# Odd layer's output product: first half of its columns spread over attention's last steps, with its weight splits inside attention

## The chip, the cores and the metric

The kernel runs on one core of one Trainium2 chip. The metric is the device time of one execution in microseconds (us). TensorE (PE), VectorE (DVE), ScalarE (ACT), GpSimd (POOL) and SyncE (SP, which here only issues DMAs) run side by side, each in the order of its own program, and meet through semaphores.

## What is computed

Two blocks of a model over 512 tokens of width 1024, in fp32. The change concerns the odd layer of the first block: differential attention with 8 heads, a normalization of each head's output, and the output product, after which comes the MLP.

```python
def diff_mixer(h, w_in, lam, subln_g, w_out, cos, sin, lambda_init):
    q, k, v = jnp.split(proj, 3, axis=-1)          # 8 heads x 2 x 64, rope on q and k
    ...
    def block(i):
        s = jnp.einsum('bqhcd,bshcd->bhcqs', qb, k) * scale
        p = masked_softmax(s, key_pos[None, :] <= tq[:, None])
        a = p[:, :, 0] - lam_val * p[:, :, 1]
        return jnp.einsum('bhqs,bshe->bqhe', a.astype(v.dtype), v)
    o = sweep_query_blocks(block, T)
    o = rms_norm(o, subln_g) * (1.0 - lambda_init)
    return jnp.einsum('bte,ed->btd', o.reshape(bsz, T, ODD_MIX), w_out)

# in first_block, layer 1
h = h + diff_mixer(...)
h = h + sq_relu_mlp(rms_norm(h, mlp_norm_g[layer]), mlp_w_up[layer], mlp_w_down[layer])
```

## The kernel before

Every fp32 product is made of three matmuls of a shorter type: each operand is split into a high part and a rest, and `products` (its matmul is line 367) adds high x high, high x low and low x high in a PSUM bank. A weight piece of 512 rows by 512 columns is loaded by SP into one of two staging buffers (`stg0`, `stg1`), ACT copies it to `wh` (L341), and DVE subtracts to get `wl` (L345). There are two `wh`/`wl` pairs too. So the split of a piece waits until TensorE has signalled "free" for the piece two before it. `split(e, key, ahead=1)` issues the split of the named piece and of the next one on engine `e`, if they haven't been issued yet. All of this stands in program order on ACT and DVE: what is behind a split waits for it.

**Attention.** 32 units n = 0 to 31: head `n // 4`, and block of 128 query rows `n % 4`, whose scores are 128, 256, 384 or 512 wide. It runs in 40 steps. In step n TensorE does, in this order: a filler, if there is one; `pe_diff_out` of unit n-3 (L1778), `pe_rows_turn` of a head, if it is due (L1828), `pe_diff_flip` of unit n-2 (L1758, transposes), `pe_diff_scores` of unit n (L1716 and the causal mask L1718). DVE takes the maximum of unit n (L1725) at the end of its step n, ACT the exponential (L1738) in step n+1, DVE the probabilities (L1746, L1748, L1750) in step n+1, ACT copies the transposed ones (L1766) in step n+2. Scores use PSUM banks 0 to 2 in turn, so those of unit n wait for exponentials of units n-2 and n-1.

**The rows of a head.** When the last unit of head hh is out, ACT squares the head (L1802, step 4hh+7), DVE sums (L1807, L1809, step 4hh+8), POOL raises to -1/2 (L1814), DVE scales (L1821, 4hh+9), TensorE transposes (L1828, 4hh+10), ACT copies the high part (L1834, 4hh+10), DVE the rest (L1838, 4hh+11). Its signal is `("rows", hh)`. The output product of head hh can start then. Head hh+2 uses the same PSUM bank, so its first `pe_diff_out` also waits for `("rows", hh)`. Below, turn(hh), copy(hh) and rest(hh) are the last three of these operations.

**Fillers.** Up to step 25 the filler is a piece of the projection of later heads (`pe_dr`), 12 matmuls in most steps. The last of it ends in step 25. After that the filler is the output product `pe_out1`: its first half of columns, c = 0, is 4 row tiles (i) by 8 heads by 3 matmuls. The heads 0 to 3 are weight piece (0,0), the heads 4 to 7 piece (0,1); the second half of columns has pieces (1,0) and (1,1). Before the change `next(out1)` gives one tile of the heads 0 to 3, 12 matmuls, in each of the steps 28, 30, 33 and 34. The heads 4 to 7 of all tiles, 48 matmuls, come after step 39: they wait for `("rows", 7)` and for the split of piece (0,1), which ACT and DVE reach only behind the rows of head 7, at the start of `act_add_norm` and `dve_add_norm`.

**Behind it.** `pe_add_norm` then runs the second half of columns in the order (heads 0 to 3: tiles 0, 1), (heads 4 to 7: tiles 0, 1), (heads 0 to 3: tiles 2, 3), (heads 4 to 7: tiles 2, 3), and the transposes of the norm. DVE adds each finished bank to `h` (L579), ACT squares it (L547). Piece (1,1) is split behind the squares of tiles 0 to 2 on ACT, when piece (0,1) is free.

Of the kernel before, what the change touches and what calls it, by code (L numbers as in the profile page):

```python
# [18 lines left out]
NT = 4  # L19
# [96 lines left out]
def build(nc, ins, out):  # L116
    ctx = ExitStack()
    with ctx:
# [10 lines left out]
        banks = ctx.enter_context(nc.psum_tensor("banks", [128, 8, 512], F32))[:, :, :]  # L129
        bank = [banks[:, i, :] for i in range(8)]  # L130
# [3 lines left out]
        rows = sb("rows", [NROWS, 128])  # L134
# [41 lines left out]

        BANKS = {"out0": (7, 0, 1, 2, 3, 4, 5, 6), "out1": (6, 7, 0, 1, 2, 3, 4, 5), "out2": (0, 1, 2, 3, 4, 5, 6, 7)}
        for tag, source in (("mlp0", "out0"), ("mlp1", "out1"), ("mlp2", "out2")):  # L180
            BANKS[tag] = BANKS[source][4:] + BANKS[source][:4]
        NORMS = {"n1": ("out0", "mlp_norm_g", 0), "n2": ("mlp0", "mix_norm_g", 8), "n3": ("out1", "mlp_norm_g", 8),
# [143 lines left out]
        def split(e, key, ahead=1):  # L326

            last = ORDER.index(key) + ahead
            while at_split[e] <= min(last, len(ORDER) - 1):
                k = ORDER[at_split[e]]  # L330
                at_split[e] += 1
                if SPEC[k][3]:
                    continue
                n = SPLITS.index(k)
                hi, lo = halves_of(k)
                if e == "act":
                    act = engine[e]
                    act.wait_ge(*piece_in[ORDER.index(k) % 2].at(k))
                    if n >= 2:
                        act.wait_ge(*p_mm.at(("free", SPLITS[n - 2])))  # L340
                    act.activation(hi, stage_of(k), ACT.Copy).then_inc(*a_hi.next(k))  # L341
                else:
                    dve = engine[e]
                    dve.wait_ge(*a_hi.at(k))
                    dve.tensor_tensor(lo, stage_of(k), hi.bitcast(F32), ALU.subtract).then_inc(*v_lo.next(k))  # L345
# [106 lines left out]
        def pe_add(pe, tag, lhs, nk, ready, free, banks=range(8), cs=range(2)):  # L452
            for c in cs:
                for g in range(nk // 4):
                    key = tag + (c, g)
                    wh, wl = take(pe, key)
                    ready(pe, g)
                    for i in range(NT):
                        if g == 0:
                            free(pe, c, i)  # L460
                        t = products(pe, bank[banks[c * 4 + i]], [(*lhs(g * 4 + k, i), wh[:, k, :], wl[:, k, :]) for k in range(4)],
                                     g == 0, g == nk // 4 - 1)
                        names = [(tag, c, i)] if g == nk // 4 - 1 else []
                        if i == NT - 1:
                            names.append(("free", key))
                        if names:
                            t.then_inc(*p_mm.next(*names))
                        yield
# [17 lines left out]

        def pe_add_norm(pe, tag, lhs, ready, free, norm, banks):
            yield from pe_add(pe, tag, lhs, 8, ready, free, banks, (0,))  # L490
            w = {}
            for x, (g, i) in enumerate(((0, 0), (0, 1), (1, 0), (1, 1), (0, 2), (0, 3), (1, 2), (1, 3))):
                if i == 0:
                    w[g] = take(pe, tag + (1, g))
                if g == 0:
                    free(pe, 1, i)
                wh, wl = w[g]
                t = products(pe, bank[banks[4 + i]], [(*lhs(g * 4 + k, i), wh[:, k, :], wl[:, k, :]) for k in range(4)],
                             g == 0, g == 1)
                names = ([(tag, 1, i)] if g else []) + ([("free", tag + (1, g))] if i == 3 else [])  # L500
                if names:
                    t.then_inc(*p_mm.next(*names))
                if norm in NORMS and x in (4, 5):
                    pe_turned(pe, norm, x - 4)
                yield
# [1215 lines left out]
        def dve_diff_max(dve, n):  # L1721
            hh, i = DIFF[n]
            for c in range(2):
                dve.wait_ge(*p_score.at(("diff", n, c)))
                dve.tensor_reduce(small[n % 16][:, c:c + 1], diff_bank(n, c)[:, 0:(i + 1) * 128], AX.X, ALU.max,  # L1725
                                  negate=True).then_inc(*v_max.next(("diff", n, c)))
# [34 lines left out]
        def act_diff_flip(act, n):  # L1761
            hh, i = DIFF[n]
            act.wait_ge(*p_flip.at(("diff", n)))
            if n >= 2:
                act.wait_ge(*p_out.at(("diff", n - 2)))
            act.activation(TDD[n % 2][:, 0:(i + 1) * 128], bank[3][:, 0:(i + 1) * 128], ACT.Copy).then_inc(  # L1766
                *a_flip.next(("diff", n)))
# [17 lines left out]
        def rows_at(n, step):  # L1785
            hh, off = divmod(n - step, 4)
            return hh if off == 0 and 0 <= hh < 8 else None
# [36 lines left out]
        def pe_rows_turn(pe, hh):  # L1824
            pe.wait_ge(*v_norm.at(("rows", hh)))
            for i in range(NT):
                s = slice(i * 128, (i + 1) * 128)
                t = pe.transpose(head_bank(hh)[:, s], OQ[:, hh % 2, s], ident)  # L1828
            t.then_inc(*p_flip.next(("rows", hh)))
# [14 lines left out]
        def first(steps, n):  # L1844
            for _ in range(n):
                next(steps, None)

        def pe_diff(pe):

            N = len(DIFF)  # L1850
            dr, out1 = pe_dr(pe), pe_out1(pe)
            first(dr, AHEAD)
            for n in STEPS:
                next(dr, None)
                if n in (N - 4, N - 2, N + 1, N + 2):
                    next(out1)
                if 0 <= n - 3 < N:
                    pe_diff_out(pe, n - 3)
                if rows_at(n, TURN) is not None:
                    pe_rows_turn(pe, rows_at(n, TURN))  # L1860
                if 0 <= n - 2 < N:
                    pe_diff_flip(pe, n - 2)
                if n < N:
                    pe_diff_scores(pe, n)
                yield
            yield from out1

        def act_diff(act):
            N = len(DIFF)
            dr, pieces = act_dr(act), act_dr_pieces(act)  # L1870
            for _ in range(AHEAD):
                first(dr, 1)
                first(pieces, 1)
            for n in STEPS:
                next(dr, None)
                if 0 <= n - 1 < N:
                    act_diff_exp(act, n - 1)
                next(pieces, None)
                if rows_at(n, SQUARE) is not None:
                    act_rows_square(act, rows_at(n, SQUARE))  # L1880
                if rows_at(n, TURN) is not None:
                    act_rows_turn(act, rows_at(n, TURN))
                if 0 <= n - 2 < N:
                    act_diff_flip(act, n - 2)
                yield

        def dve_diff(dve):
            N = len(DIFF)
            dr = dve_dr(dve)
            first(dr, AHEAD)  # L1890
            for n in STEPS:
                if rows_at(n, REST_OF) is not None:
                    dve_rows_rest(dve, rows_at(n, REST_OF))
                if 0 <= n - 1 < N:
                    if n == 1:
                        dve.wait_ge(*v_misc.at("lambda"))
                    dve_diff_prob(dve, n - 1)
                next(dr, None)
                if rows_at(n, TOTAL) is not None:
                    dve_rows_total(dve, rows_at(n, TOTAL))  # L1900
                if rows_at(n, SCALE) is not None:
                    dve_rows_scale(dve, rows_at(n, SCALE))
                if n < N:
                    dve_diff_max(dve, n)
                yield

        def pool_diff(pool):
            dr = pool_dr(pool)
            first(dr, AHEAD)
            for n in STEPS:  # L1910
# [2 lines left out]
                    pool_rows_total(pool, rows_at(n, TOTAL))  # L1913
                yield

        def pe_out1(pe):
            def lhs(k, i):
                return oTh[:, k, i * 128:(i + 1) * 128], oTl[:, k, i * 128:(i + 1) * 128]

            def ready(pe, g):  # L1920
                pe.wait_ge(*v_part.at(("rows", g * 4 + 3)))

            def free(pe, c, i):
                if c:
                    pe.wait_ge(*v_part.at(("rows", 7)))
                elif i < 2:
                    pe.wait_ge(*v_rope.at("dq7"))
                else:
                    pe.wait_ge(*a_exp.at(("diff", 31, 1)))
            return pe_add_norm(pe, ("out1",), lhs, ready, free, "n3", BANKS["out1"])  # L1930


        (nq, nk, nv, nbr), at = regions(0, [128, 4, T], [128, 4, T + 2 * META], [128, 4, T], [128, 2, 896])
# [1170 lines left out]
```

## Time and profile before

| | us |
|---|---|
| median of 3 runs | 2292.42 (2287.23 to 2292.9) |
| profiled execution | 2297.29 |
| its span on the core | 2295.5 |
| TensorE busy in the span | 2186.1 (95%) |
| DVE busy | 1058.2 (46%) |
| ACT busy | 766.3 (33%) |
| from the end of step 26 to the end of the first half of columns (964.96 to 1024.60) | 59.64, TensorE busy 44.62 |

Times within the span are counted from its start. A matmul of 512 columns shows about 0.39 us, but its successor starts 0.23 us after it, since they are pipelined; a row of the chain of waits ("x12") gives the time that the group really took. The profile's TensorE clock is 1.00 at 2.4 GHz and 0.50 at 1.2 GHz.

### The profile page before, as it was taken

The page shows a single profiled execution, that of the slowest core. Times are in us where ns is not written, and L with a number is a line of the kernel's source. Part 1 is how long each engine was busy: PE and PEld are TensorE (multiplying, and loading weights), DVE is VectorE, ACT ScalarE, POOL GpSimd, SP SyncE. Part 2 cuts the span into 40 slices and gives each one's busy share as a digit, 9 for nine tenths or more (in the row PEclk, how much of TensorE's full clock was granted, in tenths as well). Part 3 has the DMA queues.
Part 4 walks back from the last instruction along what each step waited for, and adds up shares of the span by engine and source line. Part 5 has one row for each costly group of instructions (what it writes and reads, how often), then busy time and mean ns, then how long its engine had stood idle before and what let it go on. Part 6 is the DMA issues. An engine that isn't in the chain of part 4 may idle for free.

```text
span 2295.5 us, 26641 instructions
## 1 busy us (share of the span) xinstructions
PE 2186.1 (95%) x10987; PEld 1729.6 (75%) x10987; DVE 1058.2 (46%) x1590; ACT 766.3 (33%) x1254; POOL 332.4 (14%) x308
## 2 busy tenths in 40 slices
PE   6978888999999999989999999999999999999998
PEld 5765557888888776668888888866778768888887
DVE  3568853433333456744333335355656434333333
ACT  3215453432232334434322324133423224423221
POOL 2210000111010011101200102111155320201000
PEclk9989989999999999989999999999999999999999
DMA  5430001332322321112232233221112214222321
GB/s 139 113 92 19 20 1 55 101 101 92 102 100 92 93 76 38 38 51 87 97 105 92 92 110 92 90 72 53 56 45 67 74 40 135 92 94 95 106 92 73
DMA packets 163506, 182.60 MB, mean 80 GB/s; under 512 B 19701, under 2 KB 123562, under 8 KB 163386
## 3 DMA queue, kind: packets, MB, share of 16 engines
q1 hardware_dynamic: 161066, 174.11, 24.2%
q0 software_dynamic: 2320, 6.80, 1.2%
q8 instruction: 87, 1.43, 0.3%
q14 instruction: 33, 0.27, 0.0%
HBM read 177.75 MB, written 2.17 MB: 78 GB/s over the span
## 4 chain that ended last, share of the span: by engine, by line
PE 86%; DVE 7%; ACT 3%; issue 2%; DMA 1%; SPq 1%; POOL 0%; POOLq 0%; ACTq 0%; DVEq 0%
PE banks L367 70%; PE banks L2482 2%; DVE wl L345 2%; ACT wh L341 2%; PE banks L1272 1%; PE banks L1192 1%; PE banks L1308 1%; PE banks L2601 1%; DVE uTl L537 1%; PE banks L1716 1%; PE banks L1778 1%; PE banks L2222 1%; PE banks L2172 1%; PE banks L2251 1%; PE banks L1640 1%
## 5 line engine op out<-in xcount | busy, mean ns | idle before, releaser
L367 PE MATMUL banks<-uTh,wh 128*128 128x512 f32 (+1 forms) x1408 | 555.0, 394 | 13.9 <-DVE wl L345 4.2
L367 PE MATMUL banks<-uTl,wh 128*128 128x512 f32 (+1 forms) x1408 | 539.7, 383 | 0.0
L367 PE MATMUL banks<-uTh,wl 128*128 128x512 f32 (+1 forms) x1408 | 539.6, 383 | 0.0
L367 PE MATMUL banks<-wh,hTr 128*128 128x512 f32 x1696 | 532.1, 392 | 5.5 <-DVE wl L345 4.9
L345 DVE TENSOR_TENSOR wl<-stg,wh 128x2048 fp32r<-128x2048 f32 (+1 forms) x154 | 357.2, 2320 | 385.1 <-ACT wh L341 384.6
L341 ACT ACTIVATE wh<-stg 128x2048 fp32r<-128x2048 f32 (+1 forms) x154 | 292.7, 1902 | 432.0 <-PE banks L367 399.6
L367 PEld LDWEIGHTS banks<-wh,hTr 128*128 128x128 f32 x1696 | 321.0, 189 | 73.2 <-DVE wl L345 5.3
L367 PE MATMUL banks<-wl,hTr 128*128 128x512 f32 x848 | 331.9, 391 | 0.0
L367 PEld LDWEIGHTS banks<-uTh,wh 128*128 128x128 f32 x1408 | 269.0, 191 | 70.3 <-issue 10.1
L367 PEld LDWEIGHTS banks<-uTh,wl 128*128 128x128 f32 x1408 | 268.3, 191 | 52.6
L367 PEld LDWEIGHTS banks<-uTl,wh 128*128 128x128 f32 x1408 | 269.2, 191 | 50.2 <-issue 2.4
L709 POOL TENSOR_TENSOR p<-p 128x512 f32<-128x512 f32 x96 | 109.9, 1144 | 667.5 <-ACT p L697 667.5
L720 DVE TENSOR_TENSOR hTr<-p,hTr 128x512 fp32r<-128x512 f32 x96 | 66.4, 692 | 303.2 <-ACT hTr L701 303.2
L367 PEld LDWEIGHTS banks<-wl,hTr 128*128 128x128 f32 x848 | 160.7, 190 | 33.2
L697 ACT ACTIVATE p<-banks 128x512 f32<-128x512 f32 x96 | 57.6, 600 | 202.9 <-PE banks L367 202.9
L367 PE MATMUL banks<-wh,uTh 128*128 128x512 f32 (+1 forms) x256 | 100.7, 393 | 9.9 <-DVE wl L345 6.3
L701 ACT ACTIVATE hTr<-p 128x512 fp32r<-128x512 f32 x96 | 60.7, 632 | 120.5 <-POOL p L709 120.5
L367 PE MATMUL banks<-wh,uTl 128*128 128x512 f32 (+1 forms) x256 | 98.6, 385 | 0.0
L367 PE MATMUL banks<-wl,uTh 128*128 128x512 f32 (+1 forms) x256 | 98.5, 385 | 0.0
L483 DVE TENSOR_TENSOR h<-h,banks 128x512 f32<-128x512 f32 x72 | 49.4, 686 | 82.9 <-PE banks L367 82.9
L444 POOL TENSOR_TENSOR nrm<-nrm,half 128x1 f32<-128x1 f32 x28 | 15.5, 554 | 490.8 <-DVE nrm L591 468.3
L367 PEld LDWEIGHTS banks<-wh,uTh 128*128 128x128 f32 x256 | 48.8, 190 | 20.8 <-DVE wl L345 7.0
(362 smaller groups left out, 2282.8 us busy)
## 6 DMA issues: line engine op xcount, KB each, us to landing
stg<-mlp_w_up SPq DMA_DIRECT2D x32, 1024.0 KB, 5.4
stg<-mlp_w_down SPq DMA_DIRECT2D x32, 1024.0 KB, 5.0
stg<-w_in SPq DMA_DIRECT2D x20, 1024.0 KB, 5.2
stg<-w_up SPq DMA_DIRECT2D x16, 1024.0 KB, 5.3
stg<-w_down SPq DMA_DIRECT2D x16, 1024.0 KB, 5.0
stg<-odd_w_in SPq DMA_DIRECT2D x16, 512.0 KB, 4.7
stg<-even_cmp_w SPq DMA_DIRECT2D x4, 1024.0 KB, 5.5
stg<-odd_w_in SPq DMA_DIRECT2D x4, 1024.0 KB, 5.1
```

Source lines behind the costliest of these rows:

```text
L341: act.activation(hi, stage_of(k), ACT.Copy).then_inc(*a_hi.next(k))
L345: dve.tensor_tensor(lo, stage_of(k), hi.bitcast(F32), ALU.subtract).then_inc(*v_lo.next(k))
L367: t = pe.matmul(outp, x, y, start=(start and k == 0 and m == 0), stop=(stop and k == n - 1 and m == 2))
L483: dve.tensor_tensor(hc, hc, bank[banks[c * 4 + i]], ALU.add).then_inc(*v_add.next((tag, c, i)))
L537: dve.scalar_tensor_tensor(out=uTl[:, k, s], in0=norm_rows(norm, ph, k), scalar=col(gname, g0 + k), in1=uTh[:, k, s].bitcast(F32), op0=ALU ...
L697: act.activation(P[n % 5][:, 0:T], bank[BANKS[tag][j]], ACT.Relu).then_inc(*a_up.next((tag, "relu", q, j)))
L701: act.activation(HT[q % 2][0][:, j, :], P[n % 5][:, 0:T], ACT.Copy).then_inc(*a_up.next((tag, "hi", n)))
L709: pool.tensor_tensor(r, r, r, ALU.mult).then_inc(*g_up.next((tag, n)))
L720: dve.tensor_tensor(HT[q % 2][1][:, j, :], P[n % 5][:, 0:T], HT[q % 2][0][:, j, :].bitcast(F32), ALU.subtract).then_inc(*v_up.next((tag, n)))
L1192: pe.matmul(b[:, g, :], qv[p, j, i * 128:(i + 1) * 128], kv[p, 0:w], start=True, stop=False)
L1272: t = pe.transpose(b[:, g, s], p[:, g, s], ident)
L2482: t = pe.matmul(b, fill_w["y"][:, k, f * 128:(f + 1) * 128], (onT, ohT)[br][:, k, :], start=(k == 0), stop=(k == 3))
```

## The change

- `pe_out1_half` replaces the first half of columns. The heads 0 to 3 now go in portions of 6 matmuls (two heads of a tile) or 3 (one head): tile 0 in steps 27 and 28, tile 1 in steps 29 (head 0), 30 (head 1) and 31 (heads 2, 3), tile 2 in steps 32 and 33, tile 3 in steps 34 and 35.
- The heads 4 to 6 go in 4 portions of 9 matmuls, tile 0 to 3, in steps 35 to 38. They wait for `("rows", 6)`. In step 38 the portion stands behind the transposes of head 7.
- Head 7 comes last: 4 portions of 3 matmuls, which wait for `("rows", 7)`.
- Piece (0,1) is split at the end of step 29 on ACT and DVE, piece (1,0) at the end of step 36.
- Tiles 2 and 3 change banks (1 and 0 instead of 0 and 1), and each tile waits only for what used its own bank: tile 2 for the exponential of unit 30, tile 3 for that of unit 31.

The number of matmuls stays the same.

```diff
@@ pe_diff
-                if n in (N - 4, N - 2, N + 1, N + 2):
+                if N - 5 <= n < N + 3:
                     next(out1)
                 if 0 <= n - 3 < N:
                     pe_diff_out(pe, n - 3)
                 if rows_at(n, TURN) is not None:
                     pe_rows_turn(pe, rows_at(n, TURN))
+                if N + 3 <= n < N + 7:
+                    first(out1, 2 if n == N + 3 else 1)
@@ act_diff, and the same in dve_diff, as the last thing of a step
+                if n in OUT1_SPLITS:
+                    split("act", OUT1_SPLITS[n])
@@
+        OUT1_SPLITS = {len(DIFF) - 3: ("out1", 0, 0), len(DIFF) + 4: ("out1", 0, 1)}
+        def pe_out1_half(pe):
+            w = take(pe, ("out1", 0, 0))
+            pe.wait_ge(*v_part.at(("rows", 3)))
+            for i in range(NT):
+                if i == 0:
+                    pe.wait_ge(*a_rope.at("dq7"))
+                elif i == 1:
+                    pe.wait_ge(*v_rope.at(("dq7", "sin")))
+                else:
+                    pe.wait_ge(*a_exp.at(("diff", 30 if i == 2 else 31, 1)))
+                for heads in ((0,), (1,), (2, 3)) if i == 1 else ((0, 1), (2, 3)):
+                    t = part(w, i, heads)
+                    if i == NT - 1 and heads[-1] == 3:
+                        t.then_inc(*p_mm.next(("free", ("out1", 0, 0))))
+                    yield
+            w = take(pe, ("out1", 0, 1))
+            pe.wait_ge(*v_part.at(("rows", 6)))
+            for i in range(NT):
+                part(w, i, (4, 5, 6))
+                yield
+            pe.wait_ge(*v_part.at(("rows", 7)))
+            for i in range(NT):
+                t = part(w, i, (7,))
+                t.then_inc(*p_mm.next((("out1",), 0, i), *([("free", ("out1", 0, 1))] if i == NT - 1 else [])))
+            yield
```

TensorE, between the scores of step 26 and those of step 27 (`wh0`, `wl0` are piece (0,0); `hTr_49` holds the normalized heads; `+` is the change):

```order
 L1716 MATMUL banks<-big 128x384 x2
 L1718 MATMUL banks<-causal,identb 128x128 x2
+L367 MATMUL banks<-wh0,hTr_49 128x512
+L367 MATMUL banks<-wl0,hTr_49 128x512
+L367 MATMUL banks<-wh0,hTr_49 128x512 x2
+L367 MATMUL banks<-wl0,hTr_49 128x512
+L367 MATMUL banks<-wh0,hTr_49 128x512
 L1778 MATMUL banks<-big 128x128
 L1758 MATMUL banks<-k_c_ident,p 128x128 x2
```

The first six matmuls of the output product moved to here, ahead of the `pe_diff_out` of unit 24, where nothing stood before.

TensorE, at the end of attention, steps 34 and 35 (`wh1` is piece (0,1)):

```order
 L1778 MATMUL banks<-big 128x128 x4
-L1828 MATMUL banks<-k_c_ident,big 128x128 x8
+L1828 MATMUL banks<-k_c_ident,big 128x128 x4
+L367 MATMUL banks<-wh0,hTr_49 128x512
+L367 MATMUL banks<-wl0,hTr_49 128x512
+L367 MATMUL banks<-wh0,hTr_49 128x512 x2
+L367 MATMUL banks<-wl0,hTr_49 128x512
+L367 MATMUL banks<-wh0,hTr_49 128x512
 L367 MATMUL banks<-wh1,hTr_49 128x512
 L367 MATMUL banks<-wl1,hTr_49 128x512
```

Before, the transposes of the heads 6 and 7 stand next to each other (x8); now product work stands between them, and those of head 7 come in step 38, ahead of the last portion of heads 4 to 6.

DVE, the ends of steps 29 and 36 (`sm13` belongs to unit 29; L345 is a split, `wl1` that of piece (0,1), `wl0` that of piece (1,0)):

```order
 L1821 TENSOR_TENSOR big<-banks,nrm 128x512
 L1725 TENSOR_REDUCE sm13<-banks 128x1 x2
+L345 TENSOR_TENSOR wl1<-stg1,wh1 128x2048
 L1746 RECIPROCAL sm13<-sm13 128x2
 L1748 TENSOR_SCALAR big<-big,sm13 128x256
@@ -679,8 +680,7 @@
 L1807 TENSOR_REDUCE nrm<-q1 128x4
 L1809 TENSOR_SCALAR nrm<-nrm 128x4
+L345 TENSOR_TENSOR wl0<-stg0,wh0 128x2048
 L1821 TENSOR_TENSOR big<-banks,nrm 128x512
 L1838 SCALAR_TENSOR_TENSOR hTr_49<-banks,big,hTr_49 128x512
-L345 TENSOR_TENSOR wl1<-stg1,wh1 128x2048
-L345 TENSOR_TENSOR wl0<-stg0,wh0 128x2048
```

Both splits moved from behind the last rest (L1838) to two places inside attention: one ahead of the probabilities of unit 29, one ahead of the scaling of head 7. On ACT they moved likewise, ahead of the exponentials of unit 29 and ahead of the copy of head 7.

## Rows read from the trace of the kernel before

**Rows 1.** The page, its first line: span and instructions.

```profile
span 2295.5 us, 26641 instructions
```

**Rows 2.** Stretches: length, then busy us of each engine, PEclk, DMA share, GB/s.

```profile
964.96:1024.60 59.64, 44.62 (x199) 33.71 (x199) 28.47 (x51) 19.53 (x46) 3.02 (x3) 0.80 0.11 36
...
988.00:990.00 2.00, 2.00 (x11) 1.34 (x8) 1.35 (x3) 0.36 (x2) 0.00 (x0) 0.64 0.00 0
...
994.00:996.00 2.00, 2.00 (x8) 1.59 (x7) 0.69 (x1) 0.00 (x0) 0.62 (x1) 0.65 0.00 0
...
1006.00:1008.00 2.00, 0.56 (x3) 0.16 (x1) 0.68 (x1) 1.40 (x2) 0.00 (x0) 0.50 0.00 0
```

**Rows 3.** Chain of waits, end of attention: start, us, engine, tile, line, count.

```profile
1001.38 0.70 ACT hTr L1834
...
1003.72 1.02 POOL nrm L1814
...
1005.51 1.06 PE banks L1828 x4
...
1007.18 1.91 ACT wh L341
...
1009.12 2.30 DVE wl L345
...
1011.46 26.83 PE banks L367 x108
```

**Rows 4.** TensorE in order of time: start, us, line, operation, [idle before, releaser].

```profile
962.91 0.65 PE L1828 MATMUL banks<-k_c_ident,big 128*128 128x128 f32 x4 [0.65 <-DVE big L1821]
...
968.54 0.76 PE L1778 MATMUL banks<-big 128*128 128x128 f32 x2 [3.58 <-DVE hTr L1838]
...
986.98 0.46 PE L1778 MATMUL banks<-big 128*128 128x128 f32 x2 [1.81 <-DVE hTr L1838]
...
1015.89 0.40 PE L367 MATMUL banks<-wl,hTr 128*128 128x512 f32 x1
```

**Rows 5.** Chain of waits, steps 30 to 33, where the product is a filler.

```profile
979.84 2.83 PE banks L367 x12
982.67 0.89 PE banks L1778 x8
983.56 0.44 PE banks L1828 x4
...
991.22 4.93 PE banks L367 x12
```

**Rows 6.** DVE in order of time, around the ends of steps 29 to 31.

```profile
979.67 0.68 DVE L1821 TENSOR_TENSOR big<-banks,nrm 128x512 f32<-128x512 f32 x1
980.28 0.74 DVE L1725 TENSOR_REDUCE sm<-banks 128x1 f32<-128x256 f32 x2
981.78 0.17 DVE L1746 RECIPROCAL sm<-sm 128x2 f32<-128x2 f32 x1 [0.76 <-ACT big L1738]
...
982.43 0.49 DVE L1750 SCALAR_TENSOR_TENSOR big<-big,sm 128x256 f32<-128x256 f32 x1
985.15 1.02 DVE L1725 TENSOR_REDUCE sm<-banks 128x1 f32<-128x384 f32 x2 [2.23 <-PE banks L1718]
986.09 0.74 DVE L1838 SCALAR_TENSOR_TENSOR hTr<-banks,big,hTr 128x512 fp32r<-128x512 f32 x1
```

**Rows 7.** ACT in order of time: a square, its accumulator, split of (1,1).

```profile
1022.73 0.63 ACT L547 ACTIVATE q<-h 128x512 f32<-128x512 f32 x1 [2.00 <-DVE h L579]
1023.27 0.19 ACT L547 ACTIVATION_READ_ACCUMULATOR q<-h 128x1 f32 x1
1024.79 1.92 ACT L341 ACTIVATE wh<-stg 128x2048 fp32r<-128x2048 f32 x1 [1.33 <-PE banks L367]
```

**Rows 8.** DVE in order of time: last add of the first half, split of (1,1).

```profile
1024.73 0.69 DVE L579 TENSOR_TENSOR h<-h,banks 128x512 f32<-128x512 f32 x1 [2.03 <-PE banks L367]
1026.74 2.29 DVE L345 TENSOR_TENSOR wl<-stg,wh 128x2048 fp32r<-128x2048 f32 x1 [1.32 <-ACT wh L341]
```

More of the change, by code:

```diff
@@ L175, in build @@
         xn = [PF[:, 0:D], PF[:, D:2 * D], TF[:, 0:D], TF[:, D:2 * D]]
-        BANKS = {"out0": (7, 0, 1, 2, 3, 4, 5, 6), "out1": (6, 7, 0, 1, 2, 3, 4, 5), "out2": (0, 1, 2, 3, 4, 5, 6, 7)}
+        BANKS = {"out0": (7, 0, 1, 2, 3, 4, 5, 6), "out1": (6, 7, 1, 0, 2, 3, 4, 5), "out2": (0, 1, 2, 3, 4, 5, 6, 7)}
         for tag, source in (("mlp0", "out0"), ("mlp1", "out1"), ("mlp2", "out2")):
@@ L484, in dve_add, with pe_add_norm @@
                     yield
-        def pe_add_norm(pe, tag, lhs, ready, free, norm, banks):
-            yield from pe_add(pe, tag, lhs, 8, ready, free, banks, (0,))
+        def pe_add_norm(pe, tag, lhs, ready, free, norm, banks, half=None):
+            yield from half or pe_add(pe, tag, lhs, 8, ready, free, banks, (0,))
             w = {}
@@ L1904, in dve_diff @@
                     dve_diff_max(dve, n)
+                if n in OUT1_SPLITS:
+                    split("dve", OUT1_SPLITS[n])
                 yield
@@ L1914, in pool_diff, with part @@
                 yield
+        OUT1_SPLITS = {len(DIFF) - 3: ("out1", 0, 0), len(DIFF) + 4: ("out1", 0, 1)}
+        def pe_out1_half(pe):
+            banks = BANKS["out1"]
+            def part(w, i, heads):
+                wh, wl = w
+                return products(pe, bank[banks[i]], [(*out1_rows(k, i), wh[:, k % 4, :], wl[:, k % 4, :]) for k in heads],
+                                heads[0] == 0, heads[-1] == 7)
+            w = take(pe, ("out1", 0, 0))
[22 more added lines that the diff above has]
+            yield
@@ L1916, in pe_out1, with out1_rows @@
+        def out1_rows(k, i):
+            return oTh[:, k, i * 128:(i + 1) * 128], oTl[:, k, i * 128:(i + 1) * 128]
         def pe_out1(pe):
-            def lhs(k, i):
-                return oTh[:, k, i * 128:(i + 1) * 128], oTl[:, k, i * 128:(i + 1) * 128]
             def ready(pe, g):
-                pe.wait_ge(*v_part.at(("rows", g * 4 + 3)))
+                pe.wait_ge(*v_part.at(("rows", 7)))
             def free(pe, c, i):
[L1924 to L1929, printed above, removed]
@@ L1930, in pe_out1 @@
-            return pe_add_norm(pe, ("out1",), lhs, ready, free, "n3", BANKS["out1"])
+                pe.wait_ge(*v_part.at(("rows", 7)))
+            return pe_add_norm(pe, ("out1",), out1_rows, ready, free, "n3", BANKS["out1"], pe_out1_half(pe))
         (nq, nk, nv, nbr), at = regions(0, [128, 4, T], [128, 4, T + 2 * META], [128, 4, T], [128, 2, 896])
```

## The prediction

> **What bounds the kernel now.** The page first: one execution spans 2295.5 us [rows 1], and TensorE is busy for 95% of it, so what can be won lies where TensorE waits or runs at its low clock. The view by stretches finds such a place: from the end of step 26 (964.96) to the end of the output product's first half (1024.60) pass 59.64 us, of which TensorE works 44.62 at a mean clock of 0.80 [rows 2]. It idles for 15.0 us, and the clock takes a share as well.
>
> The timeline of TensorE shows where it idles. In step 27 it waits 3.58 us and in step 31 1.81 us, both times ahead of the first `pe_diff_out` of a head, for rest(4) and rest(5) on DVE [rows 4]. The largest part comes at the end. The chain of waits reads: copy(6), rest(6) and the sums of head 7, POOL's power, the scaling, turn(7) at 1005.51, then ACT's split of piece (0,1) for 1.91 us and DVE's for 2.30 us, and only then 108 matmuls in a row from 1011.46 [rows 3]. That last link is the one to see: rest(7) isn't in the chain; the split is. From 1001.34 (end of turn(6)) to 1011.46 TensorE works 1.06 us.
>
> The clock: it is at 0.50 (1.2 GHz) in three spells, each behind idle time. The first runs from the work resumed at 968.54 to about 975, the second from about 988.7 (0.64 in the stretch 988 to 990) to about 995.4 (0.65 in 994 to 996), the third from about 1005.8 to 1015.89 (0.50 in 1006 to 1008) [rows 2, 4]. Twelve matmuls take 2.83 us at the full clock (0.23 each, taken for all portions below) and 4.93 mostly at the low one (0.43 each) [rows 5]. The excess of work done low is 3.1 us in the first spell (6.5 us of work), 3.1 in the second (6.8 less 0.56 of waiting, halved), and 2.6 in the third: 1.06 us of transposes, and ten matmuls until 1015.89 for which 4.43 us pass instead of 2.3. Together 8.8 us.
>
> The Trainium skill, "TensorE: Matmul & The Clock Gate", section Terms, gives the penalty of the low clock as the throttled time times (1 - K/N), here a half. By the stretches the clock was low for 0.20 x 59.64 / 0.50 = 23.9 us, so that rule would book 11.9 us where the rows give 8.8; the difference is idle time at the low clock, mostly in the third spell. Since the third spell goes entirely, the gain would be 2.5 us larger by the rule.
>
> **The change, step by step.** The matmuls are the same in number, and I assume that a portion of 6 costs 1.4 us. Starting a portion might cost up to 0.09 us (2.83 for x12 against 12 x 0.23) [rows 5]; four more portions stand in the steps, so between 0 and 0.4 us; I take 0 since most start behind other matmuls, and keep 0.4 for the range. I take the change through the steps against the ends of the steps before.
>
> Step 27: the first 6 matmuls run from 964.96 to 966.4, in the wait. Rest(4) on DVE is bound by DVE's own queue and doesn't move, so `pe_diff_out` still starts at 968.54 and the step ends at 971.8 as before. The idle time is 2.1 us, more than the 1.81 behind which the clock fell before [rows 4], so I let the first spell stand.
> Step 28 has 6 matmuls instead of 12, at the low clock: it ends at 976.2 instead of 977.6. Step 29 has 3 new ones and ends at 978.9 (before 979.7). Step 30 has 3 instead of 12: 0.7 + 0.89 + 0.44 [rows 5] + 1.1 for transpose and scores, to 982.1 (before 985.1). The lead is 3 us.
>
> Step 31 takes part of it back, because of the split of piece (0,1). ACT starts it behind the copy of unit 27 (978.65, as TensorE's transposes of it end at 978.0) and ends at 980.6; DVE is done with the maximum of unit 29 at 980.15 (0.74 from 979.4 [rows 6]), waits, and splits from 980.6 to 982.9. Before, DVE waited 0.76 and 2.23 us between that maximum and the next one [rows 6], so most of the 2.30 us would be covered at the old pace; at the new one it isn't. Behind the split come the probabilities of unit 29 (1.15 from 981.78 to the end of 982.43's row), the maximum of unit 30 (0.92) and rest(5) (0.74) [rows 6]: 985.7. TensorE has finished its 6 matmuls at 983.5 and waits 2.2 us for it. The step ends at 987.5 instead of 988.9. Without the split rest(5) would be ready at 983.8.
> An idle time of 2.2 us is again above 1.81, so I let a second spell of 6.6 us stand too, 1.7 us after the work resumes as before. Steps 32 and 33 (6 matmuls each, two outs, two flips) then end at 991.6 and 995.2. The exponential of unit 31 isn't waited for: its portion comes only in step 34. Before, step 33 ended at 997.2 and step 34 at 1001.34; now step 34 (6 matmuls, 8 for out, turn(6)) ends at 998.0. Lead 3.3 us.
>
> Steps 35 to 38: 6 matmuls to 999.4; rest(6) is there 1.5 us after turn(6) (0.70 [rows 3] + 0.74 [rows 6]), at 999.5. Then 9 matmuls each, to 1001.6, 1003.7 and 1005.7. Beside it runs the chain of head 7: squares to 999.3, sums to 1000.4, power 1.02 to 1001.5 [rows 3]. The split of piece (1,0) can start on ACT when (0,0) is free, at 999.4, and ends at 1001.35; DVE's ends at 1003.7, and the scaling of head 7 queued behind it ends at 1004.4 instead of 1002.2. This costs nothing, since TensorE comes to turn(7) at 1005.7. Cover: 1.3 us. Turn(7) to 1006.2, 9 matmuls to 1008.2, in which copy(7) and rest(7) (1.5 us) fit. Head 7's 12 matmuls end at 1011.0.
> Before, the 48 matmuls from 1011.46 ended at 1024.6. **Sum: 1024.6 - 1011.0 = 13.6 us.** By kinds: 15.0 us idle becomes 4.5 (2.1, 2.2, 0.15), and 8.8 us of low clock become 6.2: 13.1, with 0.5 left to rounding.
>
> What comes behind: the second half of columns starts at once with piece (1,0), split long ago. Piece (1,1) is needed after 24 matmuls, 5.5 us behind. Before, its split began with the free signal and DVE ended it 4.4 us behind 1024.6 (1026.74 + 2.29) [rows 8]. Now all four adds come in a burst of 2.1 us of matmuls, and ACT makes three squares of 0.8 us (0.63 and 0.19, overlapping a little [rows 7]) first, each behind an add (0.69 [rows 8]): the split starts 1.05 us behind, is done on ACT at 2.95 and on DVE at 5.25. The margin is 0.2 us; I take 0, at most 1. The rest of the program keeps its order.
>
> **Rivals.** *The clock holds better*: with 1.4 us of work in either wait, one of the two spells stays out, 3.1 us each: gain 16.7, or 19.8 for both. For it: step 26's wait of 0.65 us brought no spell. Against it: 1.81 us did [rows 4]. Times 2275.7 and 2272.6.
> *A split comes into the path after all*: ACT and DVE's 1.91 + 2.30 = 4.2 us [rows 3] show in full, either before turn(7), where 1.3 us cover them, or at (1,1), or in steps 30 and 31, where ACT's split also stands ahead of the exponential of unit 29 that the scores of unit 30 need. Once: gain 9.4, 2283.0; twice: 5.2, 2287.2.
> *Nothing*: the splits or products don't get their data in time and TensorE waits as before, since its chain to rest(7) rules: 2292.
> *Slower, by the clock*: the portions are short and lie between transposes and narrow products; if TensorE stays at 1.2 GHz from 968.54 on, the 33.6 us of full-clock work up to the end of the half take 67.2 and end at 1035.7, 11.1 us later than before: 2303.5. It turns the sign only if the low clock lasts 27 us longer than the 13 that I have reckoned. Before, spells in the same mix of instructions ended after 6.5 us [rows 2], so this is unlikely.
>
> **How the numbers follow.** The sum is made against the profiled execution (span 2295.5, 2297.29 in all, 1.79 outside the span). Its time is 4.87 above the median of the runs shown; the gain is in one stage and is carried over whole: 2292.42 - 13.6 = 2278.8. Chances: forecast 0.50, clock holds better 0.20, split in the path 0.20 (a quarter of it at the second price), nothing 0.05, slower 0.05. About 0.3%, 6.9 us, is what a measurement of this kernel can tell from no change. So faster 0.85, same 0.10, slower 0.05. The range leaves out "nothing" and "slower" and takes in the others: 2271 (both spells gone, 1.6 for the spread of the runs) to 2287.
>
> **What would show it.** In the profile of the changed kernel: L367 directly behind the scores of step 26; a wait of about 2 us ahead of L1778 in step 27 and of about 2 in step 31, with an L345 shortly before on DVE; no idle above 0.5 us between turn(6) and the end of the second half of columns; no split in the chain of waits between L1828 and the long row of L367; two low spells, none behind 1000. From 964.96 to the end of the first half it should be 46.0 us instead of 59.6. The prediction is wrong if TensorE waits for L345 at head 4 or at piece (1,1), if turn(7) waits for the scaling, or if a third spell shows.

## The result, and the profile after

| | before | after |
|---|---|---|
| median of 4 runs | 2291.86 us (2287.23 to 2292.90) | 2275.20 us (2268.36 to 2277.46) |
| span of the profiled execution | 2295.5 | 2274.4 |
| stage: end of step 26 to the end of the first half of columns | 59.64 | 42.75 |
| TensorE busy in the stage | 44.62 | 38.33 |

The changed kernel takes 0.9926 of the time before (95% interval 0.9901 to 0.9952): 16.7 us less by the medians, where 13.6 were forecast. A later comparison of the same kernel on another occasion gave 0.9935 (0.9918 to 0.9952).

The two profiled executions lie 21.1 us apart. The view by stretches (length, busy us of each engine, PEclk, DMA share, GB/s) of the changed kernel, cut in three, shows which part is the change:

```profile
0.00:961.05 961.05, 889.84 (x4703) 690.29 (x4708) 487.43 (x859) 345.01 (x660) 106.66 (x108) 0.97 0.26 76
961.05:1003.80 42.75, 38.33 (x198) 28.87 (x198) 28.12 (x51) 18.55 (x44) 3.02 (x3) 0.96 0.16 50
1003.80:2274.40 1270.60, 1246.61 (x6084) 1002.19 (x6083) 540.85 (x682) 403.27 (x553) 223.79 (x197) 0.99 0.26 85
```

The middle line answers to the first of [rows 2] and holds 16.9 of the 21.1 us. What follows takes 1270.6 us, and took 1270.9 (2295.5 - 1024.6) before. The first stretch is 3.9 us shorter (961.05 against 964.96), in code that the change doesn't touch: it is scatter of single executions (the same stretch takes 959.21 us in the run below whose code up to there is that of before, and between 956.6 and 963.7 in the others), and the medians don't carry it.

In the stage, TensorE's timeline (start, us, line, operation, idle before and its releaser) shows every gap that is left:

```profile
964.62 0.46 PE L1778 MATMUL banks<-big 128*128 128x128 f32 x2 [2.13 <-DVE hTr L1838]
...
979.53 0.46 PE L1778 MATMUL banks<-big 128*128 128x128 f32 x2 [2.02 <-DVE hTr L1838]
...
992.14 0.47 PE L367 MATMUL banks<-wh,hTr 128*128 128x512 f32 x1 [0.26 <-DVE hTr L1838]
...
998.38 0.60 PE L1828 MATMUL banks<-k_c_ident,big 128*128 128x128 f32 x4
```

The first two answer to [rows 4] with its 3.58 and 1.81 us; the 0.26 is the wait for rest(6); turn(7) has no wait at all. The chain of waits (start, us, what) at the same place, against [rows 3]:

```profile
990.52 0.70 ACT hTr L1834
...
991.24 0.76 DVE hTr L1838
...
992.14 6.40 PE banks L367 x27
998.54 0.44 PE banks L1828 x4
998.98 18.42 PE banks L367 x81
```

At the end of attention POOL, the scaling and both splits have left it: behind rest(6) there is only TensorE, up to the norm. One split is still in the chain, further ahead. From step 27 to the wait in step 31 the chain runs mostly through DVE and ACT and holds no filler (no L367), and both halves of the split of piece (0,1) are links of it:

```profile
972.63 1.81 ACT wh L341
...
974.46 2.29 DVE wl L345
```

TensorE also waits once where its timeline shows no gap, since short waits inside a group count as busy. The scores of unit 29 took 0.70 us before (first line) and take 1.32 in the change (second line), at the same clock:

```profile
978.92 0.70 PE L1716 MATMUL banks<-big 64*128 64x256 f32 x4
...
971.21 1.32 PE L1716 MATMUL banks<-big 64*128 64x256 f32 x4
```

The second pair of them needs a bank that unit 28 used, and the profile names the exponential (L1738) as what TensorE waits for there. TensorE comes earlier to it than before, as the low spell of step 27 is gone.

### The profile page after: what moved, and what is told of

Same layout as the page of the kernel before. It is cut to its first block, busy times and chain, and to the rows that moved or that the text cites. A ratio compares the mean times of both kernels' runs of the same rounds, so it can differ in the third digit from the quotient of the medians.

```text
span 2274.4 us, 26637 instructions
## 1 busy us (share of the span) xinstructions
PE 2174.8 (96%) x10983; PEld 1721.4 (76%) x10987; DVE 1056.4 (46%) x1590; ACT 766.8 (34%) x1254; POOL 333.5 (15%) x308
## 4 chain that ended last, share of the span: by engine, by line
PE 86%; DVE 8%; ACT 3%; issue 2%; DMA 1%; SPq 1%; POOL 0%; POOLq 0%; ACTq 0%; DVEq 0%
PE banks L367 70%; PE banks L2519 2%; DVE wl L345 2%; ACT wh L341 2%; PE banks L1272 1%; PE banks L1192 1%; PE banks L1308 1%; PE banks L2638 1%; DVE uTl L537 1%; PE banks L1716 1%; PE banks L1778 1%; PE banks L2209 1%; PE banks L2288 1%; PE banks L1640 1%; PE banks L2259 1%
## 5 line engine op out<-in xcount | busy, mean ns | idle before, releaser
L367 PE MATMUL banks<-uTh,wh 128*128 128x512 f32 (+1 forms) x1408 | 554.2, 394 | 14.1 <-DVE wl L345 4.2
L367 PE MATMUL banks<-uTl,wh 128*128 128x512 f32 (+1 forms) x1408 | 539.0, 383 | 0.0
L367 PE MATMUL banks<-uTh,wl 128*128 128x512 f32 (+1 forms) x1408 | 538.9, 383 | 0.0
L345 DVE TENSOR_TENSOR wl<-stg,wh 128x2048 fp32r<-128x2048 f32 (+1 forms) x154 | 355.4, 2308 | 382.6 <-ACT wh L341 381.9
L367 PE MATMUL banks<-wh,hTr 128*128 128x512 f32 x1696 | 530.5, 391 | 0.3 <-DVE hTr L1838 0.3
L367 PEld LDWEIGHTS banks<-wh,hTr 128*128 128x128 f32 x1696 | 318.9, 188 | 66.7 <-issue 0.7
L367 PE MATMUL banks<-wl,hTr 128*128 128x512 f32 x848 | 330.5, 390 | 0.0
L367 PEld LDWEIGHTS banks<-uTh,wh 128*128 128x128 f32 x1408 | 268.0, 190 | 70.9 <-issue 10.3
L367 PEld LDWEIGHTS banks<-uTh,wl 128*128 128x128 f32 x1408 | 267.2, 190 | 52.5
L367 PEld LDWEIGHTS banks<-uTl,wh 128*128 128x128 f32 x1408 | 268.1, 190 | 50.2 <-issue 2.4
L367 PEld LDWEIGHTS banks<-wl,hTr 128*128 128x128 f32 x848 | 159.5, 188 | 32.6
L367 PE MATMUL banks<-wh,uTh 128*128 128x512 f32 (+1 forms) x256 | 100.4, 392 | 10.9 <-DVE wl L345 6.3
L367 PE MATMUL banks<-wh,uTl 128*128 128x512 f32 (+1 forms) x256 | 98.3, 384 | 0.0
L367 PE MATMUL banks<-wl,uTh 128*128 128x512 f32 (+1 forms) x256 | 98.2, 384 | 0.0
L367 PEld LDWEIGHTS banks<-wh,uTh 128*128 128x128 f32 x256 | 48.6, 190 | 21.8 <-DVE wl L345 7.0
```

The lines of the kernel that those rows point to most:

```text
L367: t = pe.matmul(outp, x, y, start=(start and k == 0 and m == 0), stop=(stop and k == n - 1 and m == 2))
```

## Experiments

All profiles are compared over the same code. "Stage" is as above. "Long stretch" is from the scores of step 26 (L1716, 384 wide) to the first transposes of the norm (L517): 963.60 to 1038.13, so 74.53 us, before; 959.68 to 1017.24, so 57.56, in the change. A few us of one stage are at or below what the device time can tell, so the verdicts rest on profiles, and the device times stand beside them.

**The change once more.**

> The change as it is, beside the others. The stage from the end of step 26's scores to the end of the output product's first half took 59.6 us before and 42.8 after. Theory (waits of TensorE on DVE, and the low clock behind them): the stage stays at 42 to 46 us, with a wait of 2.0 to 2.2 us in step 27 and one in step 31; each may or may not bring a low spell of up to 3 us more. Rival (the 3.1 us by which the change beat the forecast of 46.0 is scatter of this one profile): a second profile shows about 46.

Measured: 2276.5 us, long stretch 57.54. The stage by stretches:

```profile
959.09:1001.80 42.71, 38.28 (x198) 28.82 (x198) 28.11 (x51) 18.51 (x44) 3.02 (x3) 0.96 0.16 50
```

It repeats to 0.04 us, with waits of 2.13 and 2.04. So 42.7 is what the change takes, and the 3 us below the forecast need a cause.

**Only the splits moved.** The kernel before, with this added at the end of the steps of ACT and DVE:

```diff
+                if n in OUT1_SPLITS:
+                    split("act", OUT1_SPLITS[n])
...
+                if n in OUT1_SPLITS:
+                    split("dve", OUT1_SPLITS[n])
...
+        OUT1_SPLITS = {len(DIFF) - 3: ("out1", 0, 0), len(DIFF) + 4: ("out1", 0, 1)}
```

These are the steps 29 and 36, as in the change.

> The kernel before, with only the two splits moved (end of steps 29 and 36); TensorE's order is that of before. Theory: a split isn't worth its own length. Piece (0,1) is ready early, but the split of (1,0) now holds the scaling of head 7 up by about 2 us with nothing on TensorE to cover it, and the 48 matmuls start behind rest(7): 59.6 - 3.4 + 2.0, a stage of 58 to 59 us, a gain of 1 to 2. Rival (the wait for the split was the cost that the change takes away): 4.2 to 4.9 us less, a stage of 55.

Measured: ratio 1.0001 (0.9991 to 1.0012), stage 58.69. TensorE's timeline at the end, against [rows 3]:

```profile
1001.42 1.11 PE L1828 MATMUL banks<-k_c_ident,big 128*128 128x128 f32 x4 [5.99 <-DVE big L1821]
1004.19 0.77 PE L367 MATMUL banks<-wh,hTr 128*128 128x512 f32 x1 [1.66 <-DVE hTr L1838]
```

The split that stood in the chain for 4.2 us is gone, and 1.0 us is all that comes of it. The wait ahead of turn(7) grew from 4.17 to 5.99 us, because the split of (1,0) now stands ahead of the scaling, and the start then waits 1.66 for rest(7). The theory's sum holds; the rival falls.

**Heads 4 to 6 behind head 7's transposes.** In the change:

```diff
-                if N + 3 <= n < N + 7:
-                    first(out1, 2 if n == N + 3 else 1)
+                if n == N + 3:
+                    next(out1)
```

> The change with one part undone: the four portions of heads 4 to 6 are no longer in steps 35 to 38 but behind step 39, ahead of head 7's. Splits and the portions of steps 27 to 35 stay. Theory: TensorE then waits for the chain of head 7 (squares, sums, power, split of (1,0), scaling, transposes, copy, rest), about 5 us ahead of turn(7) and 1.5 behind it, and a low spell follows: stage 50 to 52 us. Rival (the filling of steps 27 to 34 carries the gain, the end would be covered anyway): 43 to 45.

Measured: ratio 0.9963 (0.9948 to 0.9978), stage 49.30:

```profile
998.23 1.12 PE L1828 MATMUL banks<-k_c_ident,big 128*128 128x128 f32 x4 [4.99 <-DVE big L1821]
```

The stage by stretches:

```profile
962.40:1011.70 49.30, 40.15 (x198) 30.22 (x198) 28.14 (x51) 18.55 (x44) 3.02 (x3) 0.90 0.13 43
```

The wait of 5 us is there as forecast. The 1.5 us behind turn(7) are not: the heads 4 to 6 need only rest(6), and run directly after it. So the placement in steps 35 to 38 is worth 6.6 us of the 16.9, not 7.3 to 9.3. The rival falls too.

**Nothing in step 27.** In the change:

```diff
-                if N - 5 <= n < N + 3:
-                    next(out1)
+                if N - 4 <= n < N + 3:
+                    first(out1, 2 if n == N - 4 else 1)
```

> The change with one part undone: nothing in step 27, two portions of six in step 28. Theory: the wait in step 27 is 3.6 us again, a low spell follows it as before, and the 1.4 us of matmuls come on top in step 28: stage 1.4 + about 3 us longer than that of the change, 46.5 to 48. Rival (the low spells come at random and don't depend on the length of the wait): only the 1.4 us, 44.2.

Measured: ratio 0.9955 (0.9940 to 0.9970), stage 46.05. The stage and the 6.5 us behind the wait, by stretches:

```profile
961.70:1007.75 46.05, 40.22 (x198) 30.27 (x199) 28.32 (x51) 18.64 (x44) 3.02 (x3) 0.89 0.14 46
965.28:971.80 6.52, 6.52 (x19) 4.07 (x20) 3.34 (x8) 2.32 (x6) 0.00 (x0) 0.56 0.01 3
```

The wait is 3.58 us again and the low clock (0.56) is back behind it. The stage is 3.3 us longer, 0.5 below the range: 1.4 of it is idle time (the six matmuls don't fill the wait) and 1.9 busy time. The spell itself costs 2.6 us: from 965.28 to 972.53 pass 7.25 us, and the same matmuls take 1.77 + 2.86 = 4.6 at a clock of 1.00. In return the scores of unit 29 take 0.70 us again instead of 1.32, since TensorE comes later. That the spell came back speaks for the theory, and the next run tests it at another length.

In step 31 TensorE waits 1.99 us in this run, and a second spell follows, as in the change:

```profile
983.51 0.46 PE L1778 MATMUL banks<-big 128*128 128x128 f32 x2 [1.99 <-DVE hTr L1838]
```

The stretch from 986 to 988, where the clock (third number from the end) is 0.50:

```profile
986.00:988.00 2.00, 2.00 (x6) 1.61 (x6) 1.26 (x2) 1.30 (x4) 0.00 (x0) 0.50 0.00 0
```

**Three matmuls in step 27.** Tile 0 goes as heads 0, 1, (2, 3), one of them in step 27, two in step 28:

```diff
-                for heads in ((0,), (1,), (2, 3)) if i == 1 else ((0, 1), (2, 3)):
+                for heads in ((0,), (1,), (2, 3)) if i < 2 else ((0, 1), (2, 3)):
...
-                    next(out1)
+                    first(out1, 2 if n == N - 4 else 1)
```

> The change with 3 matmuls in step 27 and 9 in step 28. The wait in step 27 is then about 2.8 us, between the 2.1 of the change (no low spell) and the 3.6 of the kernel before (a low spell of 6.5 us). Theory (a longer wait brings the spell): it comes back, at 2.8 us, and the stage takes 45 to 46 us. Rival (what stands behind the wait decides, not its length up to 3.5): no spell, 43.4.

Measured (one run, 2282.5): stage 44.15. TensorE's timeline of steps 27 and 31:

```profile
967.23 0.77 PE L1778 MATMUL banks<-big 128*128 128x128 f32 x2 [2.82 <-DVE hTr L1838]
...
985.12 0.46 PE L1778 MATMUL banks<-big 128*128 128x128 f32 x2 [1.99 <-DVE hTr L1838]
```

Stretches of 2 us behind either of them:

```profile
969.00:971.00 2.00, 2.00 (x7) 0.63 (x4) 0.31 (x1) 0.00 (x0) 0.00 (x0) 0.50 0.00 0
...
987.00:989.00 2.00, 2.00 (x14) 1.74 (x13) 1.29 (x2) 1.22 (x3) 0.00 (x0) 1.00 0.00 0
```

At 2.82 us the spell is there again, so in this step it comes at 2.82 and 3.58 us and not at 2.13. A shorter wait always has more matmuls ahead of it here (0, 3 or 6), so these runs don't tell the length of the wait from the work before it. The stage is between the two expectations, since the second spell, behind the 1.99 us of step 31, stayed out this time. The run before had the same 1.99 us at the same place, ahead of the same matmuls, and the spell came; so it did behind the 2.02 us of the change. So the length of the wait doesn't decide alone, and what else does is open.

**The split of piece (0,1) in step 31.** In the change:

```diff
-        OUT1_SPLITS = {len(DIFF) - 3: ("out1", 0, 0), len(DIFF) + 4: ("out1", 0, 1)}
+        OUT1_SPLITS = {len(DIFF) - 1: ("out1", 0, 0), len(DIFF) + 4: ("out1", 0, 1)}
```

> The change with the split of piece (0,1) at the end of step 31 instead of 29; all else as in the change (stage 42.7 us in two profiles). Theory: the wait of 2.0 us in step 31 is caused by that split, which stands ahead of the probabilities of unit 29, the maximum of unit 30 and rest(5) on DVE. Behind step 31 the split fits in, since DVE waits there for the exponential of unit 31. Then the wait falls to about 0.3 us and the low spell behind it goes too: stage 39.5 to 40.5. Rival (DVE is full in these steps, so the split costs its 2.3 us wherever it stands): the wait moves to flip(31) or turn(6), stage 42 to 43.

Measured: ratio 0.9932 (0.9914 to 0.9950), 2276.5 us; stage 40.56, 0.06 above the theory's range. TensorE's timeline of steps 31 and 33:

```profile
977.59 0.46 PE L1778 MATMUL banks<-big 128*128 128x128 f32 x2 [0.56 <-DVE hTr L1838]
...
984.52 0.66 PE L1758 MATMUL banks<-k_c_ident,p 128*128 128x128 f32 x4 [0.71 <-DVE p L1750]
```

The stage by stretches:

```profile
960.64:1001.20 40.56, 36.90 (x198) 27.99 (x198) 28.03 (x51) 18.51 (x44) 3.02 (x3) 1.00 0.16 53
```

The wait in step 31 falls from 2.02 to 0.56 us and the clock stays at 1.00. Part of the split shows elsewhere, 0.71 us ahead of flip(31), as the rival said, but a third only. So that wait was for the most part the split's, and the place costs 2.2 us of stage (0.8 of idle time and 1.4 of low clock). The device time doesn't show it (2276.5 us, against 2275.2 and 2276.5 in the two comparisons of the change): 2 us are 0.1%. This profile also gives the stage's busy time at full clock, in the change's order: 36.9 us. It includes the 0.6 us of waiting inside the scores of unit 29.

**And step 27 filled.** Beside that:

```diff
-                for heads in ((0,), (1,), (2, 3)) if i == 1 else ((0, 1), (2, 3)):
+                for heads in ((0, 1, 2, 3),) if i == 0 else ((0,), (1,), (2, 3)) if i == 1 else ((0, 1), (2, 3)):
...
-                if N - 5 <= n < N + 3:
+                if N - 5 <= n < N + 3 and n != N - 2:
```

> As split_31, and tile 0 goes whole (12 matmuls) into step 27, tile 1's portions into steps 28, 29 and 31; step 30 has none. Theory: the matmuls that fill the wait in step 27 (2.1 us with six of them) are taken from steps in which TensorE doesn't wait, so 1.4 us come off: stage 38 to 39.2. Rival (with less filler in steps 28 and 30 TensorE waits there for exponentials): as split_31, 39.5 to 40.5.

Measured: ratio 0.9933 (0.9916 to 0.9949), 2275.5 us; stage 40.55. TensorE's timeline of steps 27, 29 and 31:

```profile
961.33 0.46 PE L1778 MATMUL banks<-big 128*128 128x128 f32 x2 [0.77 <-DVE hTr L1838]
...
968.55 0.70 PE L1716 MATMUL banks<-big 64*128 64x256 f32 x2 [0.20 <-ACT p L1738]
...
974.71 0.46 PE L1778 MATMUL banks<-big 128*128 128x128 f32 x2 [0.74 <-DVE hTr L1838]
```

The wait in step 27 fell by 1.4 us and the stage by nothing. The scores of unit 29 now wait for an exponential, step 31 waits 0.2 us more, and the busy time is 0.8 us longer at the same clock (37.7 against 36.9), in short waits that don't show as gaps: the rival was right. From step 27 to the flip of unit 31 the chain of waits of either profile holds no filler: the loop of scores, maximum, exponential and probabilities is the bound there. That is why this filler could be moved without effect.

**The split of piece (1,0) behind attention again.** In the change, `OUT1_SPLITS = {len(DIFF) - 3: ("out1", 0, 0)}`.

> The change with the second split undone: piece (1,0) is split behind rest(7) again, at the start of add_norm, not in step 36. Measured from the scores of step 26 to the first norm transposes (74.5 us before, 57.6 in two profiles of the change). Theory: on TensorE it is needed at once, so about 0.4 us of waiting there, and DVE's adds and with them the split of (1,1) come 2.3 us later than in the change, where that split had 0.5 us to spare: 1.7 us more. Together 59.5 to 60. Rival (head 7's portions and the second half's first 24 matmuls cover it): 57.6 to 58.

Measured (one run, 2276.1): long stretch 956.33 to 1015.53, so 59.20, 1.6 us more. TensorE's timeline at the first matmul with piece (1,1):

```profile
1007.23 0.50 PE L367 MATMUL banks<-wh,hTr 128*128 128x512 f32 x1 [0.94 <-DVE wl L345]
```

The last matmul of the first half and the first with piece (1,0) make a pair that takes 0.99 us instead of 0.62, because DVE isn't done with that piece:

```profile
1000.03 0.99 PE L367 MATMUL banks<-wh,hTr 128*128 128x512 f32 x2
```

Both waits of the theory are there: 0.4 us at the start of the second half, as expected, and 0.94 at (1,1) instead of 1.7. So the sum is a little below (1.6 instead of 1.9 to 2.4). The early split serves the next split, of (1,1), more than its own piece.

**Tile 2 waits for unit 31 again.** In the change, `pe.wait_ge(*a_exp.at(("diff", 31, 1)))` for tiles 2 and 3.

> The change with one part undone: tile 2, in step 32, waits for the exponential of unit 31, as before the change, though its bank was last used by unit 30. Theory: TensorE stands for about 2.1 us in step 32 (its portion starts there at 981.8, the exponential ends at 983.9), with out(29) and flip(30) queued behind, so the stretch from step 26's scores to the first norm transposes grows by 1.5 to 3 us to 59 to 60.5. Rival (the exponential of unit 31 holds the steps anyway, in flip(31)): 57.6.

Measured (one run, 2278.2): long stretch 955.23 to 1015.65, so 60.42, 2.9 us more:

```profile
979.63 0.79 PE L367 MATMUL banks<-wh,hTr 128*128 128x512 f32 x1 [2.15 <-ACT big L1738]
```

The wait is 2.15 us as computed, and the low spell lasts 6.8 us instead of 3.4, the wait included. So the finer wait is a needed part of the change. It rests on the exchange of banks, which this run leaves as it is in the change: by the code, the bank that tile 2 had before is one of unit 31's.

## Why the prediction was right, and where it was off

**The bound and the sum of idle time.** Right. 15.0 us of idle time became 42.75 - 38.33 = 4.4, forecast 4.5, in the places named: 2.13 in step 27 (2.1), 2.02 in step 31 (2.2), 0.26 for rest(6) (0.15). In step 31 both sides of the wait came earlier than forecast, TensorE by 2.1 us and DVE by 2.4, counted from the end of step 26, because the first low spell was missing; so the wait between them came out nearly as reckoned.

**Step 31 and the split.** Right, and shown by the run with the split in step 31. The chain goes as forecast: ACT's half of the split, DVE's half, the probabilities of unit 29, the maximum of unit 30, rest(5). DVE's timeline in the change, against [rows 6]:

```profile
973.62 0.75 DVE L1725 TENSOR_REDUCE sm<-banks 128x1 f32<-128x256 f32 x2
974.46 2.29 DVE L345 TENSOR_TENSOR wl<-stg,wh 128x2048 fp32r<-128x2048 f32 x1
...
977.71 1.02 DVE L1725 TENSOR_REDUCE sm<-banks 128x1 f32<-128x384 f32 x2
978.64 0.74 DVE L1838 SCALAR_TENSOR_TENSOR hTr<-banks,big,hTr 128x512 fp32r<-128x512 f32 x1
```

From the maximum of unit 29 to rest(5) there is no gap, where DVE waited 0.76 and 2.23 us before.

**Steps 35 to 38.** Right: the scaling, held up by the split of (1,0), ended 1.6 us ahead of turn(7) (at 996.8; forecast 1.3), and head 7's matmuls didn't wait. Undoing this placement costs 6.6 us, undoing the early split of (1,0) alone 1.6, at the start of the second half and at (1,1). The margin there was 0.5 us instead of 0.2. The first half ends at 1003.8, so piece (1,1) is needed at 1009.3, and DVE is done with it at 1008.7:

```profile
1006.44 2.29 DVE L345 TENSOR_TENSOR wl<-stg,wh 128x2048 fp32r<-128x2048 f32 x1 [1.92 <-ACT wh L341]
```

**The clock: the step that was off.** The prediction let both spells stand, "2.1 us, more than the 1.81 behind which the clock fell before". The first spell stayed out in all six profiles with a wait of 2.13 us in step 27, and the second lasted 3.4 us instead of 6.6. Stretches of the change behind step 27's wait and behind step 31's:

```profile
966.00:968.00 2.00, 2.00 (x12) 1.45 (x11) 1.29 (x2) 0.71 (x3) 0.00 (x0) 1.00 0.04 8
...
980.00:982.00 2.00, 2.00 (x9) 0.67 (x8) 0.90 (x3) 0.41 (x2) 0.00 (x0) 0.68 0.62 242
982.00:984.00 2.00, 2.00 (x6) 1.59 (x6) 1.25 (x2) 1.31 (x4) 0.00 (x0) 0.50 0.00 0
984.00:986.00 2.00, 2.00 (x13) 1.74 (x12) 1.76 (x4) 0.63 (x3) 0.00 (x0) 0.97 0.00 0
```

The 36.9 us that the changed order takes at full clock, less the 0.6 us of waiting in the scores of unit 29, are 36.3 us for the order before. (The other way, the matmuls of the three spells of before, set against the same matmuls at full clock in the change and in split_31, give 2.9 + 2.9 + 2.5 = 8.3 us, so again 36.3.) So the low clock cost 44.62 - 36.3 = 8.3 us before (8.8 booked) and 38.33 - 36.9 = 1.4 in the change (6.2 booked). It gave 6.9 us, not 2.6.

The second step that was off works against that. The forecast stage of 46.0 us leaves 46.0 - 4.5 - 6.2 = 35.3 us for the work at full clock, and it took 36.9: 0.5 because the low clock before was booked too dear, 0.5 in what the forecast calls rounding, and 0.6 for the wait for unit 28's exponential, which the prediction doesn't have. The clock makes the stage 4.8 us shorter than forecast and the work 1.6 longer: 46.0 becomes 42.8. So part of the closeness of 13.6 to 16.7 is luck: two misses of opposite sign.

This is the rival "the clock holds better", whose first time, 2275.7, is close to the 2275.2 measured; in the trace it is the first spell gone and half of the second.

The Trainium skill's penalty ("TensorE: Matmul & The Clock Gate", Terms: throttled time times one half here) would have booked 11.9 us before. The runs give 8.3. It overstates here, since TensorE stood idle during part of the throttled time, as in the wait of 4.90 us ahead of 1011.46, all of it at 0.50.

**The other rivals.** "A split comes into the path" did happen at one place, ahead of step 31, with 1.81 + 2.29 = 4.1 us in the chain. It cost 2.2 us of stage, not 4.2, and the wait that it makes was in the sum. "Nothing" and "slower by the clock" didn't come: there was no low spell behind 984.1, and from there on the portions between transposes ran at 1.00.

By kinds: 16.9 us of stage are 10.6 of idle time and 6.9 of low clock, less 0.6 that TensorE now waits in the scores of unit 29. By experiments: of the change's parts, the order in steps 35 to 38 is worth 6.6, step 27's portion 3.3, the finer bank wait 2.9 and the early split of (1,0) 1.6 (these two over the long stretch), each taken out alone and each from one profile. Both splits without the new order are worth 1.0 in the stage and nothing that can be measured.

## What to carry to other kernels

A split or copy that ends the chain of waits isn't worth its length: moved forward alone, it let the next chain (sums, power, scaling) surface. Look for work whose operands are ready earlier than the rest of its group, as heads 4 to 6 ahead of head 7, and put that into the wait; then the moved preparation is covered. Ask for each moved preparation what is queued behind it in strict order. And where waits on the matmul engine shrink from about 3 us to about 2, the clock may give back something too, here about two fifths of the gain, but read it from stretches of 2 us rather than from the length of one wait. Look at the length of each group of matmuls as well as at the gaps: an engine that has got ahead waits inside a group, and the profile books that as work.

## What the runs showed of the hardware

In step 27 the clock fell to 0.50 within the waits of 2.82 and 3.58 us, before the work resumed, and not in or behind those of 2.13 (six profiles) or 0.77. In step 31 it fell behind the waits of 1.81 us (two profiles), 2.02 to 2.04 (five) and 1.99 (the run with nothing in step 27), more than 1 us after the work had resumed, but not behind the 1.99 us of the run with three matmuls in step 27. So a bound in the wait's length alone isn't to be had from these runs.

Two profiled executions of the change repeat the stage to a few hundredths of a us (42.75 and 42.71), while the device times of one kernel scatter by about 10 us (2268.36 to 2277.46). Between the profiles of before and after, 3.9 us of the difference arose ahead of the stage, in unchanged code.
